# Three token groups of 2, 3 and 3 blocks in place of two of 4, sums in quads of tiles, a ring of 10 tiles

## The chip, the cores and the metric

The kernel runs on one core of a Trainium2 chip. The metric is device time in microseconds (us) of one execution; before the change it is 3839.58 us, the median of 3 runs (3836.57 to 3844.09).

## The reference

One layer over 1024 tokens (8 blocks of 128) of width 1024, all in float32:

```python
mod = silu(c) @ w_ada + b_ada                       # 6 rows: shift, scale, gate for both halves
h = modulate(rmsnorm(x, norm1_g), shift1, scale1)
qa, ka, va, qb, kb, vb, ga, gb = split(h @ w_in)
y_sb = stick_breaking_attention(qa, ka, va)         # 8 heads, strictly causal over all tokens
y_sw = sliding_window_sink_attention(qb, kb, vb)    # 2 chunks of 64, ALiBi, sinks
merged = sigmoid(ga) * (y_sb @ sb_proj) + sigmoid(gb) * (y_sw @ sw_proj)
x = x + gate1 * (merged @ w_out)
h2 = modulate(rmsnorm(x, norm2_g), shift2, scale2)
# PEER: per token and each of 8 heads, top 16 of 128 x 128 product keys
q = h2 @ w_q;  sub_s = q . sub_keys;  top 16 of each half;  top 16 of the 256 sums -> experts, gate
act = gelu(h2 . expert_u[experts])                  # 128 experts per token
x = x + gate2 * sum_k (gate * act)_k * expert_v[experts]_k
out = rmsnorm(x, final_g)
```

The expert tables have 16384 rows; a row of u and the row of v beside it are 8 KB in `uv`.

## The kernel before

There are two kinds of work. The **mixer** prepares tokens: everything up to the product keys' scores. The **stream** then fetches the experts: 1024 tiles, 128 to a block. A tile is one indirect DMA of the pool (line 498), 128 rows of 8 KB, for 32 tokens and 4 experts each. VectorE takes its dot products with the replicated h2 (line 1336), ScalarE a gelu over two tiles (line 1053), VectorE multiplies by the gate (line 1347) and spreads the weights into `dg` (line 1350), and TensorE sums the v rows with 128x32 matmuls (line 844), one group of 32 output columns for each tile of four (c = 0 to 3), into two PSUM banks. `vs_done` counts pairs of tiles. The ring in SBUF holds 8 tiles, and tile i may be fetched when the pair of tile i - 8 is summed:

```python
pool.wait_ge(vs_done, (i - RING) // 2 + 1)
```

At a change of block TensorE replicates the next h2 over the partitions (line 831), 16 times a small group of matmuls and a copy by ScalarE (line 1046); the picks of the top-k, made on VectorE in chunks of 32 tiles, are published through line 813 and lines 1030 and 1032, and `final` (lines 1361 to 1371) closes the block.

The mixer works on a group of 4 blocks, T = 512 tokens. Its stages, with the names of the plan: H (norm, transposes, line 531), V (values, line 543), then for each of 4 pairs of heads QK (line 651) and SB, the steps of the stick-breaking attention over the key blocks from the last to the first (`pair`, lines 639 to 713: scores 664, suffix sums 679 and 684, values 693; ScalarE's abs, exp, log and exp at lines 985 to 1003), SWP and SW (window attention, lines 715 to 798), MG (gates and projections, lines 567 and 570), OUT (line 596) and PREP (queries 632, key scores 616, one of 8 heads at a time). Group 0 has 4 steps to a pair, all on the diagonal; group 1 has 8. All weights are fetched once for each group, by SP. The attention's keys and values of earlier groups come back through DRAM. The adaLN modulation (line 514) has three rounds, two of them inside group 0's attention.

What sets the order: every engine has a single program, merged by `interleave` from streams that yield positions. A position is a number of tiles of the stream. `Plan` gives each item of the mixer an estimate in us and divides it by a rate in us per tile, 1.9; group 0 begins so that its PREP is at -40, group 1 at tile 40:

```python
probe = Plan(1.9, [0, 0])
length = probe.at["PREP", 0, 0] - probe.at["H", 0, 0]
at = Plan(1.9, [-length - 40, 40.0])
```

The top-k of block b, chunk m is placed by `topk_at` (line 305) at tile 32 (4b + m - 2) or when its scores are ready.

## Time and profile before

| | |
|---|---|
| median of 3 runs | 3839.58 us |
| profiled execution | 3838.94 us, span 3837.1 us |
| PE busy | 2710.1 us, 71% |
| PE weight loads | 879.3 us, 23% |
| DVE busy | 2223.6 us, 58% |
| ACT busy | 718.3 us, 19% |
| POOL busy | 1172.6 us, 31% |
| moved by DMA | 1235.07 MB, of it 1074.03 MB gathers |
| mean granted PE clock | 0.845 |

No engine is busy throughout. The span has a part without gathers, a part where gathers and the second group's mixer share the engines, and a part with gathers alone, so shares of the whole span say little; the stretches are read one by one. PE's records include two passes of every float32 matmul, and several column groups can run at once.

### The profile page before, as it was taken

To read this page: it belongs to the slowest core of one execution; us is meant where nothing else is said; L and a number is where in the kernel's file an instruction comes from. 1 tells how busy PE (TensorE), PEld (TensorE's weight loads), DVE (VectorE), ACT (ScalarE), POOL (GpSimd) and SP (SyncE) were. 2 spreads that over 40 slices of the span, in tenths; PEclk is the share of its full clock that TensorE was granted. 3 is DMA by queue.
4 is the path that set the end of the run, shared out by engine and by line. 5 is a ranking of instruction groups with operands and counts; after the bars stand their busy time and mean duration, and the time that the engine had idled before them with its cause. 6 is when DMAs were issued, how large, how long until landed. Compare 5 with 4: busy or idle time off the path is not lost. (4 is left out here: it accounts for less than half of the span.)

```text
span 3837.1 us, 33329 instructions
## 1 busy us (share of the span) xinstructions
PE 2710.1 (71%) x10216; PEld 879.3 (23%) x10216; DVE 2223.6 (58%) x5731; ACT 718.3 (19%) x1681; POOL 1172.6 (31%) x1033
## 2 busy tenths in 40 slices
PE   4886988877776777867998789655555555555555
PEld 2334433322221222222332233200110110001010
DVE  1113002458664667677776856677767767776755
ACT  1222001211435445131012211200010010001000
POOL 0000000133231333323433333444434434443443
PEclk8987999987898989988999899876777777778777
DMA  6310232699876878969998999999989989998998
GB/s 251 137 61 0 86 119 92 226 388 349 325 304 232 342 282 330 408 247 382 420 419 371 418 379 421 361 421 418 412 325 421 417 352 404 421 412 335 421 421 347
DMA packets 189067, 1235.07 MB, mean 322 GB/s; under 512 B 20348, under 2 KB 34716, under 8 KB 50392
## 3 DMA queue, kind: packets, MB, share of 16 engines
q0 software_dynamic: 147616, 1074.03, 69.2%
q1 hardware_dynamic: 41272, 158.91, 10.7%
q8 instruction: 81, 1.33, 0.1%
q14 instruction: 98, 0.80, 0.1%
HBM read 1208.71 MB, written 24.14 MB: 321 GB/s over the span
## 5 line engine op out<-in xcount | busy, mean ns | idle before, releaser
L498 POOL DMA_INDIRECT arena<-in_uv,idx_r x1024 | 1169.5, 1142 | 2639.3 <-PE pb L844 1727.9
L844 PE MATMUL pb<-arena,dg 128*32 128x512 f32 x4096 | 1288.2, 762 | 826.9 <-DVE dg L1350 826.5
L1336 DVE CUSTOM_DVE_ANT_0 arena<-arena 128x1024 f32<-128x1024 f32 x1024 | 1252.0, 1225 | 423.4 <-DMA arena<-in_uv,idx_r 398.2
L844 PEld LDWEIGHTS pb<-arena,dg 128*32 128x32 f32 x4096 | 225.9, 126 | 1780.3 <-DVE dg L1350 1251.3
L1053 ACT ACTIVATE gl<-dots 128x2 f32<-128x2 f32 x512 | 104.0, 203 | 1830.8 <-DVE dots L1336 1829.8
L1347 DVE TENSOR_TENSOR wv<-gl,gate_r 128x2 f32<-128x2 f32 x512 | 82.1, 160 | 336.2 <-ACT gl L1053 316.3
L92 ACT ACT_TABLE_LOAD x182 | 233.5, 1283 | 175.9 <-DVE dots L1336 142.1
L632 PE MATMUL pb<-arena 128*128 128x512 f32 x512 | 239.5, 614 | 12.0 <-issue 6.0
L567 PE MATMUL pb<-arena 128*128 128x512 f32 x512 | 233.2, 606 | 11.2 <-DMA arena<-in_w_mg 11.2
L831 PE MATMUL pb<-arena,ident 128*32 128x256 f32 x1024 | 98.6, 444 | 79.7 <-ACT arena L1046 75.9
L651 PE MATMUL pb<-arena 128*128 128x512 f32 x256 | 120.9, 622 | 19.3 <-DMA arena<-in_w_qk 19.3
L1220 DVE SCALAR_TENSOR_TENSOR arena<-pb,arena 128x512 f32<-128x512 f32 (+3 forms) x96 | 49.0, 552 | 139.7 <-ACT arena L995 132.1
L596 PE MATMUL pb<-arena 128*128 128x512 f32 x256 | 119.4, 617 | 14.7 <-DMA arena<-in_w_out 12.6
L632 PEld LDWEIGHTS pb<-arena 128*128 128x128 f32 x512 | 95.2, 195 | 150.1 <-issue 142.9
L567 PEld LDWEIGHTS pb<-arena 128*128 128x128 f32 x512 | 95.6, 192 | 145.4 <-issue 145.4
L1350 DVE TENSOR_TENSOR dg<-istack,wv 128x64 f32<-128x64 f32 x512 | 115.6, 226 | 19.4 <-DVE wv L1347 1.6
L1181 DVE SCALAR_TENSOR_TENSOR arena<-arena,pb 128x512 f32<-128x512 f32 x32 | 22.0, 687 | 180.9 <-PE pb L570 180.9
L570 PE MATMUL pb<-arena 128*128 128x512 f32 x256 | 116.1, 602 | 0.0
L679 PE MATMUL pb<-arena,tri 128*128 128x512 f32 (+3 forms) x192 | 85.1, 533 | 3.3 <-DVE arena L1220 3.3
L1252 DVE MAX8 vals<-arena 128x8 f32<-128x128 f32 x128 | 37.0, 289 | 84.5 <-DMA arena<-s_scratch 84.4
L1336 DVE DVE_READ_ACCUMULATOR2_ANT dots<- 128x1 f32 x1024 | 84.5, 83 | 0.0
L724 PE MATMUL pb<-arena 128*128 128x512 f32 x128 | 62.4, 640 | 17.7 <-DMA arena<-in_w_sw 17.7
(153 smaller groups left out, 2111.3 us busy)
## 6 DMA issues: line engine op xcount, KB each, us to landing
arena<-in_w_ada SPq DMA_DIRECT2D x12, 2048.0 KB, 17.5
arena<-in_w_mg SPq DMA_DIRECT2D x16, 1536.0 KB, 10.1
arena<-in_w_q SPq DMA_DIRECT2D x16, 1024.0 KB, 12.4
arena<-in_uv,idx_r POOLq DMA_INDIRECT x1024, 11.9
arena<-in_x SPq DMA_DIRECT2D x16, 512.0 KB, 13.5
arena<-in_w_qk SPq DMA_DIRECT2D x8, 1024.0 KB, 8.2
arena<-in_w_out SPq DMA_DIRECT2D x2, 4096.0 KB, 13.0
s_scratch<-arena SPq DMA_DIRECT2D x16, 512.0 KB, 15.3
```

The lines of the kernel that those rows point to most:

```text
L92: self.act.add_instruction(mybir.InstLoadActFuncSet(name=self.nc.get_next_instruction_name(), act_func_set_id=table, engine=mybir.EngineTy ...
L498: pool.indirect_dma_start(ring[:, i % RING, :], None, uv, bass.IndirectOffsetOnAxis(ap=idx_r[:, b % 2, 4 * n + c:4 * n + c + 1], axis=0)). ...
L567: m = pe.matmul(bank, wmg[ft % 2][:, q * KT + k, :], hT[:, k, :], start=(k == 0), stop=(k == KT - 1))
L570: m = pe.matmul(bank, wmg[ft % 2][:, 16 + (q - 2) * 4 + k, :], y[:, k, :], start=(k == 0), stop=(k == 3))
L596: m = pe.matmul(pb[:, BGB + 2 * (j % 2) + i, :], merged[:, k, j * P:(j + 1) * P], wout[:, k, i * HALF:(i + 1) * HALF], start=(k == 0), sto ...
L632: m = pe.matmul(pb[:, BGB + p, 0:T], wq[h % 2][:, p, k, :], h2T[:, k, :], start=(k == 0), stop=(k == KT - 1))
L651: m = pe.matmul(pb[:, BGB + i, 0:T], wqk[p % 2][:, i * KT + k, :], hT[:, k, :], start=(k == 0), stop=(k == KT - 1))
L831: x_ = pe.matmul(pb[32 * q:32 * q + 32, MISC, 256:512], selector(c), h2cur[:, 256 * i:256 * i + 256], start=True, stop=True)
L844: m = pe.matmul(pb[32 * c:32 * c + 32, VACC + i, :], dg[:, n // 2 % 2, c, :], ring[:, (2 * g + c % 2) % RING, D + i * HALF:D + (i + 1) * H ...
L1053: act.activation(gl[:, 2 * (g % 4):2 * (g % 4) + 2], dots[:, 2 * (g % 4):2 * (g % 4) + 2], ACT.Gelu).then_inc(gelu_done, 1)
L1336: dve.tensor_tensor_reduce(u, h2rep[:, c, :], u, 1.0, 0.0, ALU.mult, ALU.add, dots[:, i % 8:i % 8 + 1]).then_inc(dots_done, 1)
L1350: dve.tensor_tensor(dg[:, n // 2 % 2, 2 * (n % 2):2 * (n % 2) + 2], istack[:].unsqueeze(1).to_broadcast([P, 2, 32]), w.unsqueeze(2).to_bro ...
```

## The change

Sizes and the plan's rates:

```diff
-GROUPS = 2
-GB = NB // GROUPS
-T = GB * P
-RING = 8
+SIZE = (2, 3, 3)
+GROUPS = len(SIZE)
+FIRST = [sum(SIZE[:g]) for g in range(GROUPS + 1)]
+GROUP = [g for g in range(GROUPS) for _ in range(SIZE[g])]
+GMAX = max(SIZE)
+TMAX = GMAX * P
+RATES = (1.9, 3.1, 2.0)
+RING = 10
...
+STEP = 4
+STEPS = TILES // STEP
...
 def steps_of(g):
     out = []
-    for s in reversed(range(GB * (g + 1))):
-        lo = max(s * P - g * T, 0)
-        out.append((s, lo, s >= GB * g))
+    for s in reversed(range(FIRST[g + 1])):
+        lo = max(s - FIRST[g], 0) * P
+        out.append((s, lo, s >= FIRST[g]))
     return out
```

`Plan` takes a rate for each group, scales items by `part = SIZE[g] / 4`, and has smaller gaps:

```diff
+            self.rate = RATES[g]
             self.now = begins[g]
+            part = SIZE[g] / 4
...
-                self.item("QK", g, p, 16)
+                self.item("QK", g, p, 16 * part)
                 for i, (s, lo, diag) in enumerate(steps_of(g)):
-                    self.item("SB", g, (p, i), 2 + 6 * (T - lo) / T)
-                self.now += 3
+                    self.item("SB", g, (p, i), 2 + 6 * (SIZE[g] * P - lo) / 512)
+                self.now += 2
...
-                self.item("MG", g, f, 22)
+                self.item("MG", g, f, 22 * part)
...
-                self.item("PREP", g, h, 18)
+                self.item("PREP", g, h, 18 * part)
...
-        return self.at[stage, g, i] + later
+        return self.at[stage, g, i] + later * RATES[0] / RATES[g]
...
-        at = Plan(1.9, [-length - 40, 40.0])
+        probe = Plan([0] * GROUPS)
+        at = Plan([-probe("PREP", 0, 2) - 36, 0.0, 235.0])
...
-            ready = at("PREP", b // GB, 2 * m + 2, 5) if m < 3 else at("PREP", b // GB, 7, 16)
+            ready = at("PREP", GROUP[b], 2 * m + 1, part(GROUP[b], 11) + 4)
```

With these numbers group 0 runs from position -208 to -6, group 1 from 0 to 208, group 2 from 235 to 582; its items sum to 385, 646 and 695 us.

The stream in quads:

```diff
-                                pool.wait_ge(vs_done, (i - RING) // 2 + 1)
+                                pool.wait_ge(vs_done, (i - RING) // STEP + 1)
...
-                        for n in range(PAIRS_OF_TILES):
-                            g = PAIRS_OF_TILES * b + n
-                            yield TILES * b + 2 * n + 1.8
+                        for n in range(STEPS):
+                            g = STEPS * b + n
+                            first = STEP * n % 4
+                            yield TILES * b + STEP * (n + 1) - 0.2
                             pe.wait_ge(dg_done, g + 1)
...
                             for i in range(2):
-                                for c in range(2 * (n % 2), 2 * (n % 2) + 2):
-                                    m = pe.matmul(pb[32 * c:32 * c + 32, VACC + i, :], dg[:, n // 2 % 2, c, :],
-                                                  ring[:, (2 * g + c % 2) % RING, D + i * HALF:D + (i + 1) * HALF],
-                                                  start=(n < 2), stop=(n >= PAIRS_OF_TILES - 2))
+                                for c in range(first, first + STEP):
+                                    m = pe.matmul(pb[32 * c:32 * c + 32, VACC + i, :], dg[:, STEP * n // 4 % 2, c, :],
+                                                  ring[:, (STEP * g + c - first) % RING, D + i * HALF:D + (i + 1) * HALF],
+                                                  start=(STEP * n < 4), stop=(STEP * n >= TILES - 4))
                             m.then_inc(vs_done, 1)
...
-                    for g in range(NB * PAIRS_OF_TILES):
-                        yield 2 * g + 1.1
-                        act.wait_ge(dots_done, 2 * g + 2)
+                    for g in range(NB * STEPS):
+                        yield STEP * (g + 1) - 0.9
+                        act.wait_ge(dots_done, STEP * (g + 1))
                         table.use(GELU)
```

The gate product and `dg` on VectorE work on four tiles in the same way. The mixer's buffers are laid out for 384 tokens in place of 512, which makes room for the two tiles; matmuls, copies and DMAs take the group's own width `0:T` (256 or 384); the keys of every group but the last go to DRAM and come back for all later groups; the fetch of the norm's two rows (SCALE1, SHIFT1) of a later group also waits until the key scores of the group before are stored.

Two places show what moves. First TensorE where the stream begins, before the change. L632 and L616 are PREP's queries and key scores, L813 the picks, L831 the replication of h2, L844 the sums:

```order
L632 MATMUL pb<-arena 128x512 x16
L616 MATMUL pb<-arena 128x128 x8
L632 MATMUL pb<-arena 128x512 x16
L813 MATMUL pb<-picks,ident 32x16 x16
L616 MATMUL pb<-arena 128x128 x8
L632 MATMUL pb<-arena 128x512 x2
L831 MATMUL pb<-arena,ident 32x256 x64
L632 MATMUL pb<-arena 128x512 x6
L844 MATMUL pb<-arena,dg 32x512 x4
L632 MATMUL pb<-arena 128x512 x6
L844 MATMUL pb<-arena,dg 32x512 x4
```

And after it, where L659 and L643 are PREP, L842 the picks, L860 the replication, L558 the transposes of the next group's norm, L874 the sums, L570 its values:

```order
L659 MATMUL pb<-arena 128x256 x12
L842 MATMUL pb<-picks,ident 32x16 x16
L659 MATMUL pb<-arena 128x256 x4
L643 MATMUL pb<-arena 128x128 x4
L659 MATMUL pb<-arena 128x256 x16
L643 MATMUL pb<-arena 128x128 x4
L659 MATMUL pb<-arena 128x256 x12
L842 MATMUL pb<-picks,ident 32x16 x16
L659 MATMUL pb<-arena 128x256 x4
L643 MATMUL pb<-arena 128x128 x4
L860 MATMUL pb<-arena,ident 32x256 x64
L558 MATMUL pb<-ident,arena 128x128 x24
L874 MATMUL pb<-arena,dg 32x512 x8
```

The picks now stand 5.75 heads into PREP, in place of 4, and PREP, replication and the next group's transposes all stand ahead of the first sums.

The second place is ScalarE at a late change of block, before the change. L1053 is the gelu, L1046 the copy of the replication, L1024 the exponentials of the picks, L1030 and L1032 their publication:

```order
L1053 ACTIVATE gl<-dots 128x2 x15
L1046 ACTIVATE arena<-pb 128x256 x4
L92 ACT_TABLE_LOAD
L1024 ACTIVATE best<-best 128x32
L92 ACT_TABLE_LOAD
L1053 ACTIVATE gl<-dots 128x2
L1046 ACTIVATE arena<-pb 128x256 x4
L1030 ACTIVATE idx_r<-pb 128x4x8
L1032 ACTIVATE gate_r<-pb 128x4x8
L1046 ACTIVATE arena<-pb 128x256 x4
L1053 ACTIVATE gl<-dots 128x2
L1046 ACTIVATE arena<-pb 128x256 x4
```

And after it (L1086 the gelu, L1078 the copy, L1056, L1062 and L1064 the picks):

```order
L1086 ACTIVATE gl<-dots 128x4 x8
L1078 ACTIVATE arena<-pb 128x256 x4
L98 ACT_TABLE_LOAD
L1056 ACTIVATE best<-best 128x32
L1078 ACTIVATE arena<-pb 128x256 x4
L1062 ACTIVATE idx_r<-pb 128x4x8
L1064 ACTIVATE gate_r<-pb 128x4x8
L1078 ACTIVATE arena<-pb 128x256 x4
L98 ACT_TABLE_LOAD
L1086 ACTIVATE gl<-dots 128x4
L1078 ACTIVATE arena<-pb 128x256 x4
```

Between the copies one gelu, of the block's last four tiles, stands where two stood, behind three of the four parts of the replication.

## Rows read from the trace of the kernel before

**Rows 1.** The page: the span, and GB/s in 40 slices of it.
```profile
span 3837.1 us, 33329 instructions
...
GB/s 251 137 61 0 86 119 92 226 388 349 325 304 232 342 282 330 408 247 382 420 419 371 418 379 421 361 421 418 412 325 421 417 352 404 421 412 335 421 421 347
```
**Rows 2.** Stretches of the head: us, busy us, PEclk, DMA share, GB/s.
```profile
51.00:107.00 56.00, 38.67 (x97) 19.54 (x97) 11.40 (x12) 3.59 (x6) 0.00 (x0) 0.74 0.50 199
107.00:278.00 171.00, 142.14 (x529) 63.38 (x530) 24.23 (x76) 54.60 (x141) 0.00 (x0) 0.92 0.26 102
278.00:393.00 115.00, 75.58 (x377) 50.47 (x376) 30.94 (x56) 23.54 (x86) 0.00 (x0) 0.75 0.06 21
393.00:572.00 179.00, 166.69 (x384) 73.47 (x384) 16.52 (x24) 10.85 (x17) 0.00 (x0) 0.97 0.24 89
572.00:650.00 78.00, 62.74 (x160) 29.39 (x160) 23.60 (x28) 9.08 (x17) 0.00 (x0) 0.89 0.31 115
```
**Rows 3.** Timeline: start us, us, instruction, idle before and its releaser.
```profile
684.42 0.60 ACT L962 ACTIVATE arena<-pb 128x512 f32<-128x512 f32 x1 [0.36 <-PE pb L616]
...
716.57 0.45 PE L813 MATMUL pb<-picks,ident 128*32 128x16 f32 x32 [2.87 <-DVE picks L1312]
```
**Rows 4.** Stretches with the stream: gathers issued (x), PEclk, DMA share, GB/s.
```profile
880.00:979.00 99.00, 35.31 (x30) 0.81 0.92 356
979.00:1564.00 585.00, 180.87 (x162) 0.88 0.79 303
1564.00:1775.00 211.00, 66.87 (x60) 0.86 0.83 323
1775.00:2064.00 289.00, 108.00 (x92) 0.99 0.97 404
2064.00:2430.00 366.00, 141.01 (x123) 0.93 1.00 409
2430.00:3837.00 1407.00, 586.32 (x512) 0.75 0.96 392
```
**Rows 5.** The same for block 5 and 50 us of block 6; then timeline.
```profile
2803.00:3151.00 348.00, 142.49 (x128) 0.75 0.96 392
...
3200.00:3250.00 50.00, 20.27 (x19) 0.66 1.01 422
...
2796.96 0.94 POOL L498 DMA_INDIRECT arena<-in_uv,idx_r  x1 [11.54 <-PE pb L844]
```
**Rows 6.** Timeline: passes of 512 columns (MG) and of 128 (key scores).
```profile
408.46 7.03 PE L570 MATMUL pb<-arena 128*128 128x512 f32 x16
...
716.95 3.57 PE L616 MATMUL pb<-arena 128*128 128x128 f32 x16
```
**Rows 7.** Timeline: first scores of step 0 and of step 3, first pair.
```profile
124.62 0.49 PE L664 MATMUL pb<-arena 64*128 64x128 f32 x4 [0.69 <-ACT arena L972]
...
134.80 1.13 PE L664 MATMUL pb<-arena 64*128 64x512 f32 x4
```
**Rows 8.** Timeline: group 1's fetch of x and its first transposes.
```profile
849.60 1.82 SPq L352 DMA_DIRECT2D arena<-in_x  x4
...
880.51 1.33 PE L531 MATMUL pb<-ident,arena 128*128 128x128 f32 x8
```
**Rows 9.** Timeline: a pair's sums; weight loads of the modulation.
```profile
845.63 1.91 PE L844 MATMUL pb<-arena,dg 128*32 128x512 f32 x8
...
146.31 0.13 PEld L514 LDWEIGHTS pb<-arena,cb 128*32 128x32 f32 x4 [0.30 <-issue]
146.74 0.13 PEld L514 LDWEIGHTS pb<-arena,cb 128*32 128x32 f32 x4 [0.30 <-issue]
```
**Rows 10.** The page's DMA issues: queue, count, KB each, us to landing.
```profile
arena<-in_w_mg SPq DMA_DIRECT2D x16, 1536.0 KB, 10.1
...
arena<-in_w_q SPq DMA_DIRECT2D x16, 1024.0 KB, 12.4
```
**Rows 11.** Attention of group 1, busy us of PE, PEld, DVE, ACT, POOL.
```profile
979.00:1564.00 585.00, 425.22 (x1625) 126.78 (x1626) 362.32 (x964) 268.31 (x478) 180.87 (x162) 0.88 0.79 303
```

More of the change, by code:

```diff
@@ L109, in steps_of, with same_parity, in_slots @@
     out = []
-    for s in reversed(range(GB * (g + 1))):
-        lo = max(s * P - g * T, 0)
-        out.append((s, lo, s >= GB * g))
-    return out
+    for s in reversed(range(FIRST[g + 1])):
+        lo = max(s - FIRST[g], 0) * P
+        out.append((s, lo, s >= FIRST[g]))
+    return out
+def same_parity(b):
+    slot = [k - FIRST[GROUP[k]] for k in range(b + 1)]
+    return sum(k % 2 == slot[b] % 2 for k in slot)
+def in_slots(q, g):
+    return sum((k - FIRST[GROUP[k]]) % 2 == q for k in range(FIRST[g + 1]))
 def first_step(g):
@@ L167, in sem, with part @@
             return ctx.enter_context(nc.semaphore(name))
-        probe = Plan(1.9, [0, 0])
-        length = probe.at["PREP", 0, 0] - probe.at["H", 0, 0]
-        at = Plan(1.9, [-length - 40, 40.0])
+        probe = Plan([0] * GROUPS)
+        at = Plan([-probe("PREP", 0, 2) - 36, 0.0, 235.0])
+        def part(g, us):
+            return us * SIZE[g] / 4
         arena = sb("arena", [P, ARENA])
@@ L253, in build @@
         skt = [rows(W0 + 4096 + 256 * i, 2, NKEYS) for i in range(2)]
-        qp = rows(W0 + 4608, 2, T)
-        ssb = [f(W0 + 5632 + 1024 * i, 1024).rearrange("p (b q n) -> p b q n", b=GB, q=2) for i in range(2)]
+        qp = rows(W0 + 4608, 2, TMAX)
+        ssb = [f(W0 + 4608 + 2 * TMAX * (i + 1), 2 * TMAX).rearrange("p (b q n) -> p b q n", b=GMAX, q=2) for i in range(2)]
         dve_steps, pool_steps = sem("dve_steps"), sem("pool_steps")
@@ L259, in build @@
         in_c, in_consts, in_bias, in_g, in_sink = sem("in_c"), sem("in_consts"), sem("in_bias"), sem("in_g"), sem("in_sink")
-        in_x = [sem(f"in_x{j}") for j in range(GB)]
+        in_x = [sem(f"in_x{j}") for j in range(GMAX)]
         in_ada = [sem(f"in_ada{j}") for j in range(4)]
@@ L474, in finals @@
                         sp.dma_start(out[b * P:(b + 1) * P, :], yfin).then_inc(stored, 16)
-                interleave(start(), mods(), mixer(0), parked(0), keys(), blocks(), finals(), mixer(1), parked(1))
+                interleave(start(), mods(), mixer(0), parked(0), keys(), blocks(), finals(), *[s for g in range(1, GROUPS) for s in (mixer(g), parked(g))])
                 sp.wait_ge(stored, 16 * NB)
@@ L622, in mixer @@
                         for p in range(2):
-                            yield at("PREP", g, h, 4 * p)
+                            yield at("PREP", g, h, part(g, 4 * p))
                             if p == 0:
@@ L861, in mixer @@
                 def mixer(g):
+                    GB, T = SIZE[g], SIZE[g] * P
                     yield at("H", g, 0, -4)
                     for j in range(GB):
[L864 removed]
+                        act.wait_ge(in_x[j], 16 * sum(n > j for n in SIZE[:g + 1]))
                         if j:
[L866 to L867 removed]
+                            act.wait_ge(h_sq, FIRST[g] + j)
+                        act.activation(f(A0, D), xt[:, j, :], ACT.Square,
                                        accum_out=stats[:, j:j + 1]).then_inc(h_sq, 1)
@@ L951, in mixer @@
                         for p in range(2):
-                            yield at("PREP", g, h, 4.5 + 3.2 * p)
+                            yield at("PREP", g, h, part(g, 4 + 4 * p) + 0.2)
                             act.wait_ge(pr_q, 2 * n + p + 1)
@@ L955, in mixer @@
                                 act.wait_ge(pr_s, 2 * n + p - 1)
-                            act.activation(qp[:, p, :], pb[:, BGB + p, 0:T], ACT.Copy).then_inc(pr_qe, 1)
-                        yield at("PREP", g, h, 9.5)
+                            act.activation(qp[:, p, 0:T], pb[:, BGB + p, 0:T], ACT.Copy).then_inc(pr_qe, 1)
+                        yield at("PREP", g, h, part(g, 8.5) + 1)
                         for p in range(2):
@@ L1063, in final @@
                         act.activation(stats[:, 50:51], stats[:, 49:50], ACT.Sqrt).then_inc(fin_rstd, 1)
-                interleave(start(), gates(), replicate(), gelus(), final(), mixer(0), mixer(1))
+                interleave(start(), gates(), replicate(), gelus(), final(), *[mixer(g) for g in range(GROUPS)])
             @block.vector
@@ L1371, in final @@
                         dve.scalar_tensor_tensor(out=yfin, in0=yfin, scalar=stats[:, 50:51], in1=final_row, op0=ALU.mult, op1=ALU.mult).then_inc(fin_done, 1)
-                interleave(start(), mods(), dot_products(), weights(), keys(), final(), mixer(0), mixer(1))
+                interleave(start(), mods(), dot_products(), weights(), keys(), final(), *[mixer(g) for g in range(GROUPS)])
 def shape_constants():
```

310 lines of the change are left out of this document (160 added, 150 removed).

## The prediction

> **What bounds the kernel now.** I read the page first, then the busy time of stretches that I cut at the first instruction of each stage, then single instructions. The span is 3837.1 us [rows 1]; the profiled execution took 3838.94 us, 1.8 us more, and the median of the runs is 0.6 us above that. The sum below is made against the span. The strip of GB/s [rows 1] shows two kernels in one: for the first sixth of the span the queues are nearly idle, afterwards they move up to 421 GB/s. The stages of the mixer for blocks 0 to 3 run alone [rows 2]; PE carries them, and no tile is fetched. The first tile is issued about 718 us, right after the first picks are on PE at 716.57 [rows 3]. From there each stretch is a number of tiles [rows 4]. One tile is 128 rows of 8 KB, 1.049 MB, so 2.49 us at 421 GB/s: 1024 tiles need 2550 us of the 3119 that are left. The other 569 us are lost where the second mixer is interleaved, most of them in its attention (585 us for 162 tiles, DMA share 0.79), and at each change of block: from the first tile of a block to that of the next it is 348 us [rows 5], 29 over the 319 of the transfers. So two things set the end: when the gathers begin, and how many us a tile takes in each stretch.
>
> **The head of the program.** Before the first gather everything is on the path, and half of it goes away, as two blocks are prepared in place of four. A full-speed pass of 512 columns takes 0.44 us, and one of 128 columns 0.22, not a quarter [rows 6]; so I take 0.22 for 256 columns too. Stage by stage [rows 2]:
> - Norm and values, 51 to 107: 56 becomes 31, as the fetch of weights stays.
> - Attention, 107 to 278: 171. A pair of heads now has 32 passes of 256 columns, 7 us, and its first two steps; these ran from 124.62 to 134.80 in the old one [rows 7], 10 us; with 2 us of copies it is 19. Four pairs, 14 us for the modulation that is placed among them and 10 for the fetch of w_sw are 100.
> - Window attention, 278 to 393: 115 becomes 73 (the fetch of w_mg and the latency of the first block stay).
> - Merge, 393 to 572: 8 x 48 passes of 0.22 are 85, with 17 for the fetch of w_out 102, for 179.
> - Output, 572 to 650: 48 for 78.
>
> PREP then starts at 51 + 31 + 100 + 73 + 102 + 48 = 405. A head takes 32 x 0.22 and its scores, 8.3 us. The scores of head 1 are copied 17 us later; in the old run 32 us went from that copy (684.42) to the picks on PE [rows 3]. That gives 454, and PE, which now has 5.75 heads ahead of the picks by the order, reaches them at 453. **First gather at 456, 262 us sooner.**
>
> Not all of that counts. In the new order PE holds the rest of PREP, all replications and all transposes of the next group's norm ahead of the first sums. PREP ends at 405 + 8 x 8.3 = 471. Between the fetch of x behind PREP and the first transpose 31 us passed [rows 8]; three blocks add 10. So the first four tiles are released at about 515, and the ring of ten has been full since 486. The stream runs as if it had begun at 515 - 10 x 2.49 = **490**.
>
> **The quads.** They remove 256 visits of ACT (gelu) and 512 small instructions of DVE. On PE a pair took 1.91 us for 8 passes, two column groups at a time [rows 9]. That four groups can run at a time at 512 columns is shown by the modulation: four weights are loaded every 0.43 us [rows 9]. So a quad costs about 1.9 us as a pair did: 0.48 for 0.95 us a tile. Under a stream bound by DMA this is worth nothing by itself; it counts where PE is full. A quad is released late, but the ring grew: with 8 and pairs, six tiles are still under way or waiting at a release; with 10 and quads also six, 15 us of transfers. Hence I give the larger ring no gain in steady state. At a change of block ACT and PE serve 16 replications, and the pool waits 11.5 us for a release [rows 5]. In the new order the last four tiles wait for all of them, but four places are then freed at once and ten tiles are under way. I count six tiles in store at the last dot, 15 us, and a release at about 19: some 6 to 8 us of idle DMA, and 6 us of a block's other transfers, in place of 29. **15 us less at three changes in the tail, 20 us for the four others, where mixers hide part: 65.** Bounds: 0 and 150.
>
> **The interleaved stretches.** The plan now gives group 1 its 646 us at 3.1 per tile, 208 tiles, and group 2 its 695 at 2.0, 347 tiles; 27 tiles lie between, 442 behind. For each old stretch the floor is its tiles plus its loads at 421 GB/s, and the ratio of time to floor [rows 4] is what I carry over: norm and values 99/85 = 1.16; attention 585/421 = 1.39; window 211/158 = 1.33; merge 289/259 = 1.12; output and PREP 366/346 = 1.06. A group fetches all weights again: 12.6 MB of w_mg, 8.4 of w_q [rows 10] and some 18 of others, 39 MB and 92 us, now twice beside the stream.
> - Group 1 (14.6, 59.7, 29.1, 42.6 and 62.3 tiles): floors 45, 169, 81, 136, 193; times 52, 254, 117, 156, 205, together **784**. Attention is at 1.5, window at 1.45 and merge at 1.15, since there is more mixer to a tile and its chains show more.
> - Group 2: floors 60, 336, 116, 194, 264; times 70, 444, 154, 217, 280, **1165**. Attention is at 1.32, as it has 25% fewer columns for four tiles a step; 1.25 gives -24, 1.39 +23.
> - Between: 27 x 2.66 = **72**. Tail: 442 x 1407/512 = **1215** [rows 4].
>
> PE, at full clock, needs in group 1 some 490 us of mixer (144 passes of 0.43, 848 of 0.32, attention 78, small ones 77) and 208 x 0.58: 611, below 784. ACT was busy 268 of 585 us in the old attention [rows 11], and has fewer table loads to make. So neither is a bound at the old clock.
>
> Sum: 490 + 784 + 1165 + 72 + 1215 - 65 = 3661; with 2.4 us around it **3663 us**, 4.6% faster.
>
> The trace moves 422 GB/s for 50 us at a time [rows 5]. The Trainium skill (DMA: Bandwidth & Descriptors, Where 436 GB/s comes from) says instead that HBM limits a core to about 358; by that the 1024 tiles would take 3000 us and the sum would be about 4110. By that rule the old kernel could not have ended at 3837, so the trace disagrees.
>
> **Rivals.** A difference of 0.2%, 8 us, is what a measurement can tell from none.
> - *My forecast*, 3600 to 3740, bounds of attention and of the block changes included: **0.62**.
> - *The mixer's time adds up rather than hides.* Take each old stretch as a share of (mixer alone + tiles alone), alone by [rows 2] and columns: 0.76, 0.9 (585 of 247 + 403), 0.8, 0.74 and 0.72. Group 1's sums are 78, 299, 157, 228 and 310, so 846; group 2's 93, 524, 192, 286 and 381, so 1182; without the gain at block changes 3805: range 3740 to 3847. For it: chains through three in-order engines, and group 1 has more mixer per tile. Against: half as many visits. **0.20**, a sixth of it within 0.2% of before.
> - *The stream comes close to its floor*, since quads take PE and ACT time from every stretch: ratios of 1.15 in attention and window of both groups take 160 us off, 3500: range 3450 to 3600. **0.11**. For it: 256 fewer rendezvous. Against: softmax chains alone nearly fill group 1's attention.
> - *Slower: PE runs at its low level in group 1.* Narrow passes with waits for weights and chains between them let the granted clock fall. It decides where 611/c exceeds 784 by 185, at a mean c of 0.63. At 0.56 it is 1091, and the kernel takes 3970. Against: no interleaved stretch was under 0.81, and dense ones were at 0.99 [rows 4]. **0.06**. The Trainium skill (TensorE: Matmul & The Clock Gate, HAM oscillation) says that thin matmuls that alternate with waits for DMA keep falling back to the low clock, and speaks against narrower groups; the old tail (0.75) and the head's window stage (0.75) agree, the merge does not.
>
> That the stream waits for group 1's picks instead (block 2 needs them at tile 256, the plan ends at 208) has 0.01, at 3850.
>
> **Numbers.** Range 3575 to 3785: all of the forecast, two thirds of the second case, a little of the third. Faster by over 0.2% 0.90, within 0.2% 0.04, slower 0.06.
>
> **What would show it.** First gather at 440 to 475 and first release about 515: else the head is wrong. 235 to 290 us for the 60 tiles of group 1's attention; 330 to 336 us for a block in the tail; the 16 passes of a quad's sums in 1.9 us at full clock: if they take 3.6 there, the four groups don't run together. DMA busy for 39 MB more. It is wrong if group 1 takes over 850 us, or if its granted clock is under 0.8.

## The result and the profile after

The changed kernel takes **3718.71 us** (median of 3 runs, 3715.27 to 3719.81) in place of 3839.58: the ratio is 0.9682, with a 95% interval of 0.966 to 0.9704, so 3.2% faster. The forecast was 3663 us, range 3575 to 3785. The time lies in the range, 56 us above the forecast.

The page of the kernel after, for the span, the busy times and the queues:

```profile
span 3716.9 us, 34683 instructions
...
PE 2262.8 (61%) x11240; PEld 998.4 (27%) x11240; DVE 2161.4 (58%) x5280; ACT 685.8 (18%) x1587; POOL 1137.3 (31%) x1033
...
GB/s 261 171 72 164 194 214 300 340 330 287 315 370 372 362 403 324 352 369 374 355 354 355 422 421 339 374 420 419 351 396 421 417 338 421 421 420 335 421 421 338
...
q1 hardware_dynamic: 48456, 199.80, 13.8%
```

The stream begins in the fifth slice of forty, where it began in the eighth [rows 1]. The hardware queue moves 199.80 MB, 41 more than before (158.91 MB): the weights of a third group, forecast as 39. The same stretches as before were cut at the first instruction of each stage: H and V, attention, window, merge, output with PREP of group 1; the gap; the same five of group 2; the tail. Only the first stretch is cut otherwise: it begins at 508, where the stream would have begun had it never waited (533.3 less ten tiles of 2.49 us), and the norm's first transpose is at 513.9. Columns: us, busy us of PE, PEld, DVE, ACT and POOL, PEclk, DMA share, GB/s.

```profile
508.00:572.00 64.00, 36.09 (x128) 15.45 (x128) 45.04 (x106) 6.76 (x14) 14.68 (x12) 0.71 0.58 229
572.00:792.00 220.00, 165.17 (x760) 73.51 (x760) 133.31 (x358) 102.24 (x221) 68.23 (x60) 0.89 0.81 318
792.00:908.00 116.00, 72.62 (x464) 44.62 (x464) 77.02 (x178) 28.39 (x84) 29.74 (x28) 0.79 0.76 298
908.00:1093.00 185.00, 159.83 (x721) 80.03 (x722) 99.73 (x236) 22.58 (x54) 46.03 (x44) 0.95 0.86 340
1093.00:1313.00 220.00, 184.40 (x776) 91.53 (x776) 115.49 (x274) 36.66 (x73) 65.75 (x60) 0.90 0.92 359
1313.00:1395.00 82.00, 23.74 (x144) 4.52 (x144) 51.40 (x125) 9.68 (x21) 30.45 (x27) 0.64 1.01 415
1395.00:1475.00 80.00, 54.33 (x296) 19.20 (x296) 48.50 (x108) 13.53 (x31) 25.54 (x21) 0.73 0.89 353
1475.00:1880.00 405.00, 292.75 (x1385) 113.28 (x1385) 284.06 (x722) 188.88 (x382) 141.86 (x128) 0.85 0.91 358
1880.00:2019.00 139.00, 88.49 (x577) 46.82 (x577) 106.67 (x258) 39.15 (x101) 51.31 (x44) 0.81 0.84 334
2019.00:2224.00 205.00, 167.74 (x704) 81.50 (x704) 134.94 (x333) 16.80 (x42) 72.66 (x64) 0.92 1.01 421
2224.00:2518.00 294.00, 223.57 (x1064) 99.95 (x1064) 178.40 (x419) 51.10 (x107) 97.92 (x89) 0.86 0.94 380
2518.00:3717.00 1199.00, 449.40 (x2545) 82.14 (x2544) 795.25 (x1918) 92.75 (x239) 480.57 (x438) 0.58 0.95 393
```

These rows answer to [rows 2, 4]. The stages of group 0 start at 49.4, 80.5, 185.9, 245.6 and 344.8, PREP at 391.6. Beside the forecast:

| stretch | forecast | measured | error |
|---|---|---|---|
| begin of the stream, as if it had never waited | 490 | 508 | +18 |
| group 1 | 784 | 805 | +21 |
| between | 72 | 82 | +10 |
| group 2 | 1165 | 1123 | -42 |
| tail, with 15 us less at each of three changes of block | 1170 | 1199 | +29 |
| the four other changes of block | -20 | in the rows above | +20 |

The sum of the errors is 56 us. It hides larger ones that cancel: how, only the experiments show.

**The head.** The first gather is issued at 446.4 (forecast 456), but the pool's next wait is long. The timeline after PREP, where the ring is full (start us, us, instruction, idle before it and its releaser):

```profile
485.45 0.36 ACT L1078 ACTIVATE arena<-pb 128x256 f32<-128x256 f32 x1
...
487.45 1.08 PE L860 MATMUL pb<-arena,ident 128*32 128x256 f32 x8 [0.50 <-ACT arena L1078]
488.60 0.38 ACT L1078 ACTIVATE arena<-pb 128x256 f32<-128x256 f32 x1 [1.20 <-PE pb L860]
...
511.16 1.28 DVE L1142 SCALAR_TENSOR_TENSOR arena<-arena,stats 128x1024 f32<-128x1024 f32 x1 [25.21 <-ACT stats L903]
...
528.79 3.64 PE L874 MATMUL pb<-arena,dg 128*32 128x512 f32 x16 [1.28 <-DVE dg L1386]
...
533.27 1.39 POOL L524 DMA_INDIRECT arena<-in_uv,idx_r  x1 [74.70 <-PE pb L874]
```

Between 485 and 509 ACT and PE pass 16 pieces of the replicated h2 to each other, 1.58 us each, with PE at half clock (granted clock 0.50 from 485 to 509). The Sqrt of group 1's norm stands behind them on ACT, DVE waits 25 us for it, and in the order of every engine the first sums stand behind that norm and its transposes. So the first release is at 533, not at 515.

**A change of block in the tail.** The timeline of the changed kernel: a replication of h2 ahead of the change, the block's last dot product, a replication after it, and the pool's two waits:

```profile
3358.84 0.64 PE L860 MATMUL pb<-arena,ident 128*32 128x256 f32 x8 [0.50 <-ACT arena L1078]
...
3364.32 1.22 DVE L1371 CUSTOM_DVE_ANT_0 arena<-arena 128x1024 f32<-128x1024 f32 x1
...
3372.07 1.08 PE L860 MATMUL pb<-arena,ident 128*32 128x256 f32 x8 [0.50 <-ACT arena L1078]
...
3385.05 0.94 POOL L524 DMA_INDIRECT arena<-in_uv,idx_r  x1 [22.78 <-PE pb L874]
...
3396.89 1.19 POOL L524 DMA_INDIRECT arena<-in_uv,idx_r  x1 [6.13 <-PE pb L874]
```

The pool waits 22.8 and 6.1 us, for four places each. Before the change it waited for two places each time: the 11.5 us of [rows 5], and then 12.3 and 5.6 us. The second of these three:

```profile
2811.44 0.94 POOL L498 DMA_INDIRECT arena<-in_uv,idx_r  x1 [12.30 <-PE pb L844]
```

The changed kernel's release comes 19.5 us after the end of the last dot product (3365.5), and 19 were forecast. But the tiles in store, forecast as 15 us of transfers, last only 6. Stretches, columns as above:

```profile
3366.00:3372.00 6.00, 3.88 (x56) 1.19 (x56) 0.00 (x0) 1.48 (x6) 0.00 (x0) 0.50 0.91 381
3372.00:3385.00 13.00, 9.40 (x64) 2.00 (x64) 2.83 (x8) 3.70 (x9) 0.00 (x0) 0.56 0.02 8
```

DMA is idle for 13 us, where 6 to 8 were forecast; at the same change before, it was idle for about as long in two pieces (shares of 0.09 and 0.35 in 8 us each, from 3487 and from 3499). A block of the tail takes 345 us, in place of 348 before; 330 to 336 were forecast. A part of the wait is PE's clock: the passes of a replication take 1.08 us here and 0.64 a little earlier, at full clock, and nine replications lie between the last dot product and the sums. An estimate from these numbers and the sums' 3.14 us (1.9 at full clock) is some 5 us of the 19.5.

The ledger is this: the stream starts 272 us earlier, and the end comes only 120 us earlier.

### The profile page after: what moved, and what is told of

Read it like the earlier page. It is cut to its first block and busy times, and to the rows that moved or that the text cites. A ratio compares the mean times of both kernels' runs of the same rounds, so it can differ in the third digit from the quotient of the medians.

```text
span 3716.9 us, 34683 instructions
## 1 busy us (share of the span) xinstructions
PE 2262.8 (61%) x11240; PEld 998.4 (27%) x11240; DVE 2161.4 (58%) x5280; ACT 685.8 (18%) x1587; POOL 1137.3 (31%) x1033
## 3 DMA queue, kind: packets, MB, share of 16 engines
q1 hardware_dynamic: 48456, 199.80, 13.8%
## 5 line engine op out<-in xcount | busy, mean ns | idle before, releaser
L874 PE MATMUL pb<-arena,dg 128*32 128x512 f32 x4096 | 757.7, 878 | 946.1 <-DVE dg L1386 939.0
L874 PEld LDWEIGHTS pb<-arena,dg 128*32 128x32 f32 x4096 | 136.0, 140 | 1466.0 <-DVE dg L1386 1159.7
L1086 ACT ACTIVATE gl<-dots 128x4 f32<-128x4 f32 x256 | 52.4, 205 | 1347.0 <-DVE dots L1371 1346.1
L659 PE MATMUL pb<-arena 128*128 128x384 f32 (+1 forms) x768 | 253.4, 488 | 60.2 <-DMA arena<-in_sk 32.9
L594 PE MATMUL pb<-arena 128*128 128x384 f32 (+1 forms) x768 | 238.0, 465 | 27.5 <-DMA arena<-in_w_mg 27.5
L1383 DVE TENSOR_TENSOR wv<-gl,gate_r 128x4 f32<-128x4 f32 x256 | 41.2, 161 | 308.8 <-ACT gl L1086 275.9
L659 PEld LDWEIGHTS pb<-arena 128*128 128x128 f32 x768 | 154.3, 206 | 151.1 <-issue 78.0
L594 PEld LDWEIGHTS pb<-arena 128*128 128x128 f32 x768 | 147.8, 195 | 115.9 <-issue 49.5
L860 PE MATMUL pb<-arena,ident 128*32 128x256 f32 x1024 | 109.4, 509 | 71.7 <-ACT arena L1078 62.2
L623 PE MATMUL pb<-arena 128*128 128x512 f32 x256 | 123.2, 635 | 48.4 <-DMA arena<-in_w_out 47.5
L679 PE MATMUL pb<-arena 128*128 128x384 f32 (+1 forms) x384 | 128.0, 492 | 38.4 <-DMA arena<-in_w_qk 38.4
L1255 DVE SCALAR_TENSOR_TENSOR arena<-pb,arena 128x384 f32<-128x384 f32 (+2 forms) x120 | 51.7, 472 | 145.5 <-ACT arena L1027 124.4
L597 PE MATMUL pb<-arena 128*128 128x384 f32 (+1 forms) x384 | 116.8, 455 | 0.0
L679 PEld LDWEIGHTS pb<-arena 128*128 128x128 f32 x384 | 78.0, 208 | 90.7 <-DMA arena<-in_w_qk 41.4
L707 PE MATMUL pb<-arena,tri 128*128 128x384 f32 (+2 forms) x240 | 95.0, 489 | 8.7 <-DVE arena L1255 8.1
L597 PEld LDWEIGHTS pb<-arena 128*128 128x128 f32 x384 | 72.6, 191 | 45.0 <-issue 9.8
L721 PE MATMUL pb<-arena 128*64 128x384 f32 (+2 forms) x240 | 62.9, 467 | 31.9 <-ACT arena L1035 28.9
```

What stands on the lines that cost most here:

```text
L594: m = pe.matmul(bank, wmg[ft % 2][:, q * KT + k, :], hT[:, k, 0:T], start=(k == 0), stop=(k == KT - 1))
L597: m = pe.matmul(bank, wmg[ft % 2][:, 16 + (q - 2) * 4 + k, :], y[:, k, 0:T], start=(k == 0), stop=(k == 3))
L623: m = pe.matmul(pb[:, BGB + 2 * (j % 2) + i, :], merged[:, k, j * P:(j + 1) * P], wout[:, k, i * HALF:(i + 1) * HALF], start=(k == 0), sto ...
L659: m = pe.matmul(pb[:, BGB + p, 0:T], wq[h % 2][:, p, k, :], h2T[:, k, 0:T], start=(k == 0), stop=(k == KT - 1))
L679: m = pe.matmul(pb[:, BGB + i, 0:T], wqk[p % 2][:, i * KT + k, :], hT[:, k, 0:T], start=(k == 0), stop=(k == KT - 1))
L707: m = pe.matmul(pb[:, BGB + c % 4, 0:T - lo], tri[:], spl[:, c % 4, 0:T - lo], start=False, stop=True, skip_group_check=True)
```

## The experiments

Runs were made in three batches, each on another chip, with the kernel before in each of them: 3827.47 us beside the first four kernels below, 3827.84 beside quads_ring10, quads_pe_twice, visits_by_pair and replicate_early, and 3847.57 beside the last four. Kernels of different batches are therefore compared by their ratio to it. "Block 0 to 5" is the time from the first dot product of block 0 to that of block 5, which holds both interleaved mixers; "two blocks of the tail" is from there to the first of block 7.

### Quads and ring apart

Four kernels, each the changed one with one or two numbers set back, and the changed one once more. The last of the four has the old groups with quads; it keeps the other new gaps of the plan, and in it, as in mixers_stretched, the `link(op)` that ties the top-k's instructions together stands ahead of a `yield` and not behind it.

```diff
-STEP = 4
+STEP = 2          # pairs_ring10, pairs_ring8
-RING = 10
+RING = 8          # quads_ring8, pairs_ring8, two_groups_quads8
-SIZE = (2, 3, 3)
+SIZE = (4, 4)     # two_groups_quads8, with the old rates and begins
```

> The changed kernel with sums, gelu and gate product in pairs of tiles again (STEP = 2), ring of 10 kept. Theory A (the gain is the earlier start; quads relieve PE, ACT and DVE a little in the interleaved stretches): 3735 to 3775 us, 20 to 55 above the changed kernel's 3719, with first gather unchanged at 446 and blocks of the tail at 345. Rival B (quads are only a cost, as a quad is released late, and a ring of 10 in pairs keeps eight tiles under way): under 3710 us.

> The changed kernel with a ring of 8 tiles, quads kept: at a release only four tiles are still fetched or waiting, 10 us of transfers, less than the 12 us from issue to landing. Theory A (the two tiles more pay for the quads): 3900 us or more, the tail at 390 us a block or more. Rival B (the ring is slack): within 15 us of 3719.

> The three groups alone: pairs and ring of 8 as before the change. Theory A (the start is worth 210 us of base, of which the third fetch of weights and the denser group 1 take 80 to 110 back): 3740 to 3790. Rival B (without quads PE and ACT can't carry group 1 at 3.1 us of mixer per tile): over 3830, group 1's attention at over 280 us.

> Two groups of 4 blocks as before, at rate 1.9 each, with quads in a ring of 8 (10 don't fit beside buffers for 512 tokens). Theory A: like quads_ring8, late releases cost in every stretch bound by transfers: 3950 us or more. Rival B (quads relieve the engines and the ring is slack): 3780 to 3830.

> The changed kernel itself, beside its parts on the same chip. From its first dot product of block 0 to that of block 5 it took 2173 us, where pairs in a ring of 10 took 2297; its period in the tail was 345. If the two-by-two of quads and ring holds, 3700 to 3720 us here: 113 to 133 less than pairs with a ring of 10 (3833) and 134 to 154 less than quads with a ring of 8 (3854).

| kernel | us | ratio, 95% interval | block 0 to 5 | two blocks of the tail | table loads |
|---|---|---|---|---|---|
| before | 3839.58 | 1 | 2076 | 695 | 182 |
| pairs_ring8 | 3863.76 | 1.0092, 1.0075 to 1.0109 | 2322 | 689 | 231 |
| pairs_ring10 | 3833.05 | 1.0019, 1.0008 to 1.003 | 2297 | 679 | 231 |
| quads_ring8 | 3853.88 | 1.0072, 1.0055 to 1.0089 | 2210 | 752 | 178 |
| quads_ring10 | 3712.69 | 0.9695, 0.9672 to 0.9718 | 2168 | 689 | 178 |
| two_groups_quads8 | 3920.63 | 1.025, 1.0233 to 1.0267 | 2067 | 748 | 150 |

The first row is the run of the result section. Theory A missed all four times: quads_ring8 and two_groups_quads8 came out below its 3900 and 3950, the two kernels with pairs above its ranges. Of the rivals only one came near: pairs_ring8 is over 3830, as Rival B said, but its attention of group 1 took 262 us (571 to 833) and not over 280. Theory A had valued quads and ring at 65 us, and the groups at the rest. quads_ring10 came out inside its 3700 to 3720.

**The three groups alone are a loss**, 0.9%. The first dot product comes 214 us sooner (727 to 513), but blocks 0 to 5 take 246 us more. The rows of the whole stretch say why, before and pairs_ring8 (columns as above):

```profile
727.00:2803.00 2076.00, 1569.70 (x6204) 500.94 (x6198) 1381.57 (x3616) 499.86 (x1081) 732.16 (x639) 0.88 0.91 362
```
```profile
513.00:2835.00 2322.00, 1799.82 (x7404) 710.20 (x7408) 1419.59 (x3700) 625.30 (x1376) 708.51 (x638) 0.89 0.87 337
```

What left the head, the mixer of two blocks, now runs beside the stream: 230 us more of PE and 125 more of ACT, and DMA's share falls from 0.91 to 0.87. The stretch also moves some 31 MB more (337 GB/s over 2322 us, 362 over 2076), the weights of one more group, 74 us at 421 GB/s; these the forecast had. The runs don't say how much of the 246 each takes. The mixer's time was not hidden. Ring and quads **pay only together**: the ring alone gives 31 us, the quads alone 10, both 151. The table shows the two halves. Quads take 112 us (ring of 8) or 129 (ring of 10) from blocks 0 to 5. In the tail they cost 63 us for two blocks in a ring of 8 and 10 in a ring of 10. Inside a block of the tail, quads_ring8 and then quads_ring10 (columns as above):

```profile
3140.00:3440.00 300.00, 96.78 (x521) 16.45 (x512) 199.41 (x495) 14.88 (x42) 116.06 (x108) 0.56 0.97 381
```
```profile
3070.00:3330.00 260.00, 94.42 (x509) 16.68 (x512) 185.92 (x466) 14.47 (x40) 110.62 (x100) 0.60 1.01 419
```

With eight places a release frees half the ring, and 381 GB/s are moved where ten places give 419. The pool's own wait for a release is hardly longer (6.0 and 5.0 us on average, of 27 and 25 waits), so the fewer tiles in store are the likelier cause; no run separates the two.

**Quads help the old groups as well.** Blocks 0 to 5 of two_groups_quads8 take only 9 us less than before, but that is a gain and a loss. Its attention of group 1:

```profile
970.00:1488.00 518.00, 360.39 (x1616) 117.39 (x1616) 346.36 (x860) 224.93 (x409) 183.44 (x159) 0.86 0.86 336
```

That is 67 us less than the 585 of [rows 11] for nearly as many gathers (159 and 162), with 65 us less of PE and 43 us less of ACT. The stretch of gathers alone from the end of PREP to block 5 takes 426 us for 144 gathers, where it took 373 for 134: there the quads pay for the ring of 8. (Smaller gaps of the plan are in this kernel too, so the 67 us are not the quads' alone.) A ring of 10 with the old groups was not run, since it doesn't fit.

### What in the quads gives the 129 us

At the same clock a quad halves PE's time for the sums (two column groups at a time become four; 757 us in place of 1250 over the program) and halves the visits of ACT and DVE. First try, the order of a quad's eight matmuls:

```diff
-for i in range(2):
-    for c in range(first, first + STEP):
+for c, i in ((0, 0), (1, 0), (1, 1), (2, 0), (2, 1), (3, 0), (3, 1), (0, 1)):
```

> The changed kernel with the eight passes of a quad in an order in which only two column groups can run at a time, so that a quad costs PE four steps in place of two, 0.95 us a tile as pairs did, while ACT and DVE are visited as rarely as before. Theory P (the quads' gain of 124 us up to block 5 is the PE time that they save): block 0 to block 5 takes 2270 to 2310 us in place of 2173, the total is 3800 to 3840. Theory V (it is the visits of ACT and DVE and the waits between engines, half as many): 2170 to 2195 and a total within 25 us of the changed kernel.

Measured: 3707.51 us, ratio 0.9684 (0.9663 to 0.9705). That says nothing of either theory, since the edit didn't do what it was to do. A quad's sums in quads_pe_twice, and in quads_ring10:

```profile
538.54 1.94 PE L874 MATMUL pb<-arena,dg 128*32 128x512 f32 x16 [0.44 <-DVE dg L1386]
```
```profile
537.32 1.92 PE L874 MATMUL pb<-arena,dg 128*32 128x512 f32 x16 [0.28 <-DVE dg L1386]
```

So both halves were made again, by other means. The sums issued twice with half weights, `stack = 0.5 * np.tile(...)`:

```diff
-for i in range(2):
+for i, r in ((0, 0), (1, 0), (0, 1), (1, 1)):
```

and gelu and weights by pairs of tiles with the sums by quad, the waits counted to match:

```diff
-for g in range(NB * STEPS):
-    yield STEP * (g + 1) - 0.9
-    act.wait_ge(dots_done, STEP * (g + 1))
+for g in range(NB * STEPS * 2):
+    yield 2 * (g + 1) - 0.9
+    act.wait_ge(dots_done, 2 * (g + 1))
```

> The changed kernel in which PE does the 16 passes of each quad twice (with weights of half the size, so the sums come out the same): 3.84 us a quad at full clock, the 0.96 us a tile of pairs, and the visits of ACT and DVE stay those of quads. Gelu and weights by pair took 59 us of the 124 that quads save up to block 5. Theory P (the other 65 are PE's time): block 0 to block 5 takes 2225 to 2250 us in place of 2168, the total is 3765 to 3795. Theory V (the other 65 are the second visit of PE, the waits of the mixer behind it): 2168 to 2190, total within 25 us of 3713.

> The mirror of the run before: gelu and weights are made for each pair of tiles, 256 visits of ACT and 512 small DVE instructions more, and the sums of PE are issued for the quad at once, four column groups at a time, so PE's time is that of the changed kernel. Theory P: block 0 to block 5 takes 2170 to 2195 us, the total is within 20 us of the changed kernel. Theory V: 2250 to 2300, total 3780 to 3830.

| kernel | us | ratio, 95% interval | block 0 to 5 | busy PE sums | table loads |
|---|---|---|---|---|---|
| quads_ring10 | 3712.69 | 0.9695, 0.9672 to 0.9718 | 2168 | 757 | 178 |
| visits_by_pair | 3784.11 | 0.9891, 0.9866 to 0.9915 | 2227 | 756 | 231 |
| sums_twice | 3862.18 | 1.0035, 1.0023 to 1.0047 | 2312 | 1233 | 178 |
| pairs_ring10 | 3833.05 | 1.0019, 1.0008 to 1.003 | 2297 | 1250 | 231 |

Both cost, so neither theory alone is right. The expectations missed: 2227 us lies between the ranges of the two theories (only the total of 3784 is in Theory V's), and 2312 is above both ranges of sums_twice. The profiled execution of sums_twice, 3878 us, is the slowest of its eight. The visits cost 71 us in all. The attention of group 2, 128 tiles, shows what they are made of; rows by line of quads_ring10 (1475 to 1880 us):

```profile
L874 PE MATMUL pb<-arena,dg 128*32 128x512 f32 x512 | 89.5, 833 | 86.3 <-DVE dg L1386 86.3
L98 ACT ACT_TABLE_LOAD x56 | 71.8, 1283 | 53.6 <-DVE dots L1371 52.6 <-DVE stats L1404 0.4
```

visits_by_pair (1495 to 1937 us):

```profile
L98 ACT ACT_TABLE_LOAD x92 | 118.0, 1283 | 55.0 <-DVE dots L1371 53.4 <-DVE stats L1404 0.4
L874 PE MATMUL pb<-arena,dg 128*32 128x512 f32 x512 | 91.8, 854 | 95.9 <-DVE dg L1386 95.9
```

sums_twice (1553 to 2002 us):

```profile
L874 PE MATMUL pb<-arena,dg 128*32 128x512 f32 x1024 | 152.5, 749 | 77.4 <-DVE dg L1386 77.4
L98 ACT ACT_TABLE_LOAD x56 | 71.8, 1283 | 47.5 <-DVE dots L1371 46.5 <-DVE stats L1404 0.4
```

A gelu between the logarithms and exponentials of the attention needs another function table, and so does the next logarithm: 36 more loads of 1.283 us, 46 us, and the stage takes 442 us in place of 405. Over the program it is 53 loads, 68 us of ACT, beside the 71 measured. The loads were not varied apart from the visits' other cost, so that they are nearly all of it is argued from these counts. In sums_twice ACT is as in the changed kernel, PE has 63 us more in this stage, and the stage takes 449. To the end the doubled sums cost 3.4% (1.0035 in place of 0.9695), some 130 us. Going back to pairs altogether costs 120 (pairs_ring10), less than 71 and 130 together, so the two costs don't add. That ACT's loads are hidden while PE is late, and the other way round, would explain it, but no run shows it. The doubled sums also hold a quad's four places longer, which this run doesn't tell apart.

### The start

The 16 replications of block 0 are put between the heads of PREP (the line shown is ACT's, PE's is moved likewise), its h2 is fetched earlier, and group 1 begins 8 tiles later, behind the first two quads' sums:

```diff
-yield TILES * b - 3.5 + c + 0.1 * i if b else -2
+yield TILES * b - 3.5 + c + 0.1 * i if b else -38 + 4 * c + i
-at = Plan([-probe("PREP", 0, 2) - 36, 0.0, 235.0])
+at = Plan([-probe("PREP", 0, 2) - 36, 8.0, 235.0])
```

> The changed kernel with the 16 replications of block 0 moved from behind PREP of group 0 to between its heads, h2 of block 0 fetched earlier for them, and group 1 begun 8 tiles later, so that the sums of the first two quads stand ahead of group 1's squares on ACT. Theory A (the chain of replications, squares and the norm's Sqrt on ACT holds the first release at 533): the first release comes at 475 to 485, right behind PREP, tile 10 is issued about 50 us sooner and the total falls by 35 to 55 us. Theory B (the time is given back in group 1, whose mixer and not the stream sets the pace): the first release is as early but the total falls by less than 15 us, and the first dot of block 2 comes when it did.

Measured: 3683.6 us, ratio 0.9617 (0.9594 to 0.964), 29 us less. The first release, POOL's timeline:

```profile
503.41 1.05 POOL L524 DMA_INDIRECT arena<-in_uv,idx_r  x1 [34.49 <-PE pb L874]
```

It comes at 503, 30 us earlier and not 50. The next wait is on DVE, whose timeline shows the first dot product, and the second behind a chunk of the top-k that waits for its scores:

```profile
475.24 1.22 DVE L1371 CUSTOM_DVE_ANT_0 arena<-arena 128x1024 f32<-128x1024 f32 x1
...
491.58 0.29 DVE L1287 MAX8 vals<-arena 128x8 f32<-128x128 f32 x1 [15.11 <-DMA arena<-s_scratch]
...
492.41 1.22 DVE L1371 CUSTOM_DVE_ANT_0 arena<-arena 128x1024 f32<-128x1024 f32 x1
```

But what was won at the first release arrived at the end: 30 us there, 29 in the total, and the first dot product of block 2 comes 28 us earlier (1441 in place of 1469). So Theory B falls. Theory A's mechanism holds, but both its numbers missed: the release came at 503 and not by 485, and the total fell by 29 us and not by 35 to 55. Early replications and the later begin of group 1 were changed together, so the run doesn't say what each is worth.

### A larger ring in the tail

From tile 600 on, once PREP of group 2 is stored, 8 more tiles lie in the mixer's part of the arena:

```diff
+def slot(i):
+    return i % RING if i < WIDE0 else (i - WIDE0) % WIDE     # WIDE0, WIDE = 600, 18
...
+if i == WIDE0 + RING:
+    pool.wait_ge(s_st[0], 16 * HEADS // 2 * GROUPS)
+    pool.wait_ge(s_st[1], 16 * HEADS // 2 * GROUPS)
```

> The changed kernel with a ring of 18 tiles from tile 600 on: the mixer's part of the arena is free once PREP of group 2 is done, and 8 more tiles lie there. Theory S (in the tail a block takes 345 us because the pool waits for a release at the change of block, 23 and 6 us of it): the period of blocks 5 to 7 falls to 322 to 330, the total to 3645 to 3670. Theory T (a transfer that starts later runs faster in return, so the stream has no slack to win; the 345 are what the DMA queues give): 340 to 345, total above 3700.

> Both edits together: the replications of block 0 inside PREP (29 us won alone) and the ring of 18 in the tail. If the two gains add up: 3713 - 29 - (what tail_ring18 wins), 3615 to 3645 under Theory S; near 3680 under Theory T.

> As the run before, with the two interleaved mixers spread over more tiles: rates 2.65 and 1.83 in place of 3.1 and 2.0, group 2 begun at tile 262 in place of 235 (and the ring of 18 from tile 660). Theory M (in group 1 the mixer's chains set the pace, DMA share 0.81 in its attention, so more tiles fit beside each stage at no cost): the total falls by another 20 to 60 us. Theory O (each stage's time is the sum of its mixer and its tiles, so that the order of the mixing is worth nothing): within 15 us of the run before, or slower, since less of the tail has the ring of 18.

Measured: tail_ring18 3680.28 us, ratio 0.9564 (0.9541 to 0.9586), which is 1.3% or 50 us below the changed kernel's 0.9695. Part of the 50 lies in the comparison of two chips: from block 5 to the end the trace of tail_ring18 takes 991 us and that of quads_ring10 1029, 37 less, and up to block 5 the two take nearly the same (2173 and 2168). Both edits together take 3652.99 us, 0.9491 (0.9475 to 0.9507), 2.0% below: the gains of 0.8 and 1.3% add up, and on the same chip as tail_ring18 the early replications give 27 us. Block 5 in tail_ring18, and in the changed kernel; block 6 takes 331 and 345 us:

```profile
2686.00:3019.00 333.00, 130.75 (x772) 24.44 (x776) 237.79 (x596) 29.03 (x74) 144.86 (x128) 0.62 1.01 419
```
```profile
2687.00:3032.00 345.00, 130.61 (x772) 24.34 (x768) 238.19 (x594) 28.83 (x73) 137.44 (x128) 0.57 0.96 397
```

The engines do the same work in less time. The 13 us at the change to block 7, in which DMA was idle in the changed kernel, now look like this:

```profile
3345.00:3358.00 13.00, 9.42 (x64) 1.92 (x64) 2.88 (x8) 3.68 (x8) 0.00 (x1) 0.55 0.94 393
```

The pool still waits 23 to 24 us there, but 14 tiles are under way or in store, and of the gap some 2 us are left. The period is 332, a little above the 322 to 330 expected; the total is above the 3645 to 3670 as measured and inside them by the ratio (0.9564 of the 3828 us of the second batch is 3661). Theory T falls.

The last run spreads the mixers over more tiles (the ring of 18 then from tile 660):

```diff
-RATES = (1.9, 3.1, 2.0)
+RATES = (1.9, 2.65, 1.83)
```

It took 3645.1 us, 0.9468 (0.9452 to 0.9484). The total is 8 us below the run before, which is Theory O's outcome, and 0.2% is within the intervals. It is the sum of two effects: blocks 0 to 5 take 2170 us in place of 2190, about the least that Theory M expected, but block 5, where the mixer now lasts longer and the large ring comes later, takes 349 in place of 331. That the order of the mixing is worth nothing is therefore not shown. It has the lowest median of all: 5.3% below the kernel before and 2.3% below the changed one.

## Why the prediction was right, and where only by its sum

- **The head** (stages, first gather at 456): the gather came at 446.4. Right to 10 us. **First release about 515**: 533. The step that failed is the count of what stands between PREP and the first sums: norm and transposes were there, the 16 replications at half clock, 25 us on ACT ahead of the norm's Sqrt, were named but not priced.
- **"The interleaved stretches", group 1 at 784.** Here pairs are the fair test, as the ratios came from pairs. Group 1 took 866 us in pairs_ring10 (508 to 1374): 64, 256, 115, 202, 229 by stage. Attention and window were right (254, 117), merge (156) and output with PREP (205) were not. The rows of pairs_ring10 for these two:

```profile
943.00:1145.00 202.00, 181.53 (x720) 82.99 (x720) 104.53 (x267) 24.40 (x65) 45.78 (x44) 0.96 0.81 314
1145.00:1374.00 229.00, 210.51 (x776) 93.26 (x776) 119.04 (x302) 38.82 (x86) 66.47 (x59) 0.93 0.92 351
```

PE is busy 0.90 and 0.92 of them. In the attention no engine is: PE 198 of 256 us, ACT 126, DVE 139, and yet DMA's share is 0.74:

```profile
572.00:828.00 256.00, 197.69 (x760) 76.64 (x760) 138.66 (x391) 126.35 (x252) 62.83 (x60) 0.89 0.74 275
```

My check, 611 us of PE against 784, was made over the whole group; stage by stage PE alone needs 182 us where I forecast 156. Group 2 in pairs was 34 us over its 1165 (459 for 444 in attention). The rival "the mixer's time adds up" had 846 for group 1, and is nearer than my forecast for the sum, though not for attention (0.9 of its 299, so 269). The changed kernel itself, with quads, took 220 us for that attention, below the 235 to 290 of the signs.
- **"The quads ... worth nothing by itself under a stream bound by DMA".** This is the step that was most wrong, as no interleaved attention was bound by DMA (share 0.79 in [rows 4]). Quads in a ring of 10 are worth 129 us up to block 5. PE's time for the sums and the visits of ACT and DVE both have a part in it; the runs don't divide it cleanly. In the old groups too the attention was 67 us shorter with quads. I had written that ACT "has fewer table loads to make" and gave them no price.
- **"I give the larger ring no gain in steady state."** With pairs it is worth 31 us, with quads 141: without it the stream waits for every quad. "With 10 and quads also six" tiles is a right count of places, and for 8 and quads the same count gives four. So no gain over the old kernel was a fair term for both together, but it hid that quads without the ring are worth next to nothing.
- **15 us less at each change of block in the tail:** 3 us. The last quad's gelu stands behind three of the four replication parts, and all four places wait for it. That mechanism was seen, and its time was right: 19 us forecast from the last dot product to the release, 19.5 measured. The term that was mis-sized is the store, "six tiles in store at the last dot, 15 us": the transfers ran out after 6 us, so DMA was idle for 13 and not for 6 to 8.
- **The other rivals:** no low clock in group 1 as a whole, where the granted clock is 0.88 from 508 to 1313. It is 0.71 in the short norm, 0.79 in the window attention, a little under the 0.8 of the signs, and 0.89 to 0.95 elsewhere, so "slower" didn't come by that way. Near the floor no stage of the mixer came but the merge of group 2 (421 GB/s). In the tail the granted clock fell from 0.75 to 0.58, with PE busy 449 of 1199 us, where it had been 783 of 1407. The Trainium skill (TensorE: Matmul & The Clock Gate, HAM oscillation) says that thin matmuls between waits for DMA keep falling back to the low clock. The tail agrees. Inside a block of the tail this costs nothing that the rows show (419 GB/s at a clock of 0.60), but at a change of block it is a part of the wait, the 5 us estimated above.
- **HBM.** tail_ring18 moves 419 GB/s over a whole block of 333 us. The Trainium skill (DMA: Bandwidth & Descriptors, Where 436 GB/s comes from) has about 358 as HBM's limit for a core, half of what a stack gives to two. So again the trace disagrees, with one core at work; no run here shows two. The prediction's own argument against it was too short: 1024 tiles in 3000 us from 718 on would end at 3718, before 3837. What excludes 358 here is the 392 GB/s over the 1407 us of the old tail [rows 4].

Two errors cancelled in part. With pairs, from which the ratios of the interleaved stretches came, the trace of pairs_ring10 is 164 us above the forecast: 18 at the start, 122 in the interleaved stretches (82 + 6 + 34), 20 at the other changes of block and 4 in the tail. Quads took 108 of them back (124 up to block 5, less 16 after it), and they were not in the sum. What is left is 56. That the time lies in the range is therefore partly luck: without quads' gain it would have been 3833, outside it. The direction held because all parts were in the change: of the four kernels with three groups, with pairs or quads in a ring of 8 or 10, three are no faster than the kernel before.

## What to carry to other kernels

Work that is moved from a serial head beside a stream is not free by itself: add up each engine's busy time stage by stage, not over the group, and count function table loads as work of ACT. Where a stage is a chain through several engines, even busy shares well below 1 don't show room. A coarser release needs a larger ring, and the one is worth little without the other; memory that falls free when a phase ends can give the later phase its ring. What was won before the first release of the stream, with the mixing behind it nearly unchanged, arrived at the end (29 of 30 us).

## What was not expected of the hardware

- Another order of a quad's eight matmuls made no difference: with two of them in turn on the same 32 columns (and different PSUM banks) the 16 passes took 1.94 us, in place of 1.92. Only this one other order was run.
- A table load took 1.283 us every time. Splitting 256 gelus into 512 made 53 more of them.
- A replication of 256 columns at half clock took 1.58 us, of which 1.08 are PE's passes and 0.38 ACT's copy; nothing overlaps, since one PSUM region is handed to and fro. At full clock the passes took 0.64 and the whole 1.14.
